# A hybrid decoder step on one core: norm inputs without a scaled copy, other orders at the seams between layers, and a routing stage whose norm, row scaling and gather are cut differently

## What is computed

```python
def rmsnorm(x, g):
    xf = x.astype(F32)
    y = xf * lax.rsqrt(jnp.mean(xf * xf, axis=-1, keepdims=True) + EPS) * g.astype(F32)
    return y.astype(x.dtype)

def short_conv_mix(xn, buf, w_in, conv_w, w_out):
    b, c, h = jnp.split(xn @ w_in, 3, axis=-1)
    u = c * h
    ...
    return (b * y) @ w_out, u_ext[:, -(CONV_W - 1):]

def swiglu(x, w1, w3, w2):
    return (jax.nn.silu(x @ w1) * (x @ w3)) @ w2

def moe_swiglu(x, router, w1, w3, w2):
    logits = (xt @ router).astype(F32)
    top_v, top_i = lax.top_k(logits, TOP_K)
    gates = jax.nn.softmax(top_v, axis=-1)
    ...
    for e in range(N_EXPERTS):
        out = out + combine[:, e:e + 1] * swiglu(xt, w1[e], w3[e], w2[e]).astype(F32)
```

## Time and profile before

| what | value |
|---|---|
| median of 3 runs | 1589.92 us (1587.15 to 1593.22) |
| the profiled execution's own time | 1587.53 us |
| its span | 1585.8 us |
| PE busy (matmul) | 1499.7 us, 95% |
| DVE busy | 1239.5 us, 78% |
| ACT busy | 954.3 us, 60% |
| POOL busy | 66.5 us, 4% |
| HBM | 305 GB/s over the span |

### The profile page before, as it was taken

The page is one execution under the profiler, slowest core; times in us unless marked ns, Lnnn a source line. Parts: engine busy times, 40 slices in busy tenths (PEclk is TensorE's granted clock), DMA queues, the critical chain, the costliest instruction groups (busy, mean ns, idle before and its releaser), DMA issues.

```text
span 1585.8 us, 23285 instructions
## 1 busy us (share of the span) xinstructions
PE 1499.7 (95%) x8758; PEld 1307.8 (82%) x8759; DVE 1239.5 (78%) x886; ACT 954.3 (60%) x671; POOL 66.5 (4%) x61
## 2 busy tenths in 40 slices
PE   6998699999989979999999999999999999999992
PEld 5987689999979978888888888888888888888881
DVE  5898665655657759888888888888888888888883
ACT  4644244334334347777777777777777777777761
POOL 1033400000000011000000000000000000000001
PEclk9999899999989989999999999999999999999997
DMA  7645377888726539999999999999999999999962
GB/s 269 194 154 163 124 280 268 297 312 312 248 102 200 167 99 400 395 393 374 377 380 370 377 379 370 377 384 360 389 375 362 383 382 357 385 381 362 380 240 96
DMA packets 212938, 484.49 MB, mean 306 GB/s; under 512 B 8810, under 2 KB 26314, under 8 KB 209820
## 3 DMA queue, kind: packets, MB, share of 16 engines
q1 hardware_dynamic: 209080, 473.67, 82.4%
q10 hardware_dynamic: 2532, 5.84, 1.0%
q0 software_dynamic: 1280, 4.33, 0.7%
HBM read 446.45 MB, written 37.40 MB: 305 GB/s over the span
## 4 chain that ended last, share of the span: by engine, by line
PE 82%; DVE 4%; issue 1%; ACT 1%; DMA 1%; POOL 0%; POOLq 0%; ACTq 0%; DVEq 0%
PE Q L2166 20%; PE Q L2122 13%; PE Q L2120 13%; PE Q L2121 13%; PE Q L1737 7%; PE Q L1738 7%; PE Q L1739 7%; PE Q L2151 2%; DVE wlo L1020 1%; DVE sr L1054 0%; PE Q L2101 0%; DMA back<-y_rows,idx 0%; PE Q L2130 0%; DVE xl L1046 0%; DVE xn L1041 0%
## 5 line engine op out<-in xcount | busy, mean ns | idle before, releaser
L1020 DVE TENSOR_TENSOR wlo<-raw,whi 128x2048 fp32r<-128x2048 f32 x414 | 940.3, 2289 | 207.0 <-ACT whi L887 121.1
L887 ACT ACTIVATE whi<-raw 128x2048 fp32r<-128x2048 f32 x336 | 643.1, 1921 | 185.0 <-PE Q L2122 85.4
L2120 PE MATMUL Q<-whi,xgh 128*128 128x512 f32 x896 | 357.5, 399 | 2.4 <-issue 2.4
L2122 PE MATMUL Q<-whi,xgl 128*128 128x512 f32 x896 | 353.8, 395 | 0.0
L2121 PE MATMUL Q<-wlo,xgh 128*128 128x512 f32 x896 | 352.8, 394 | 0.0
L1737 PE MATMUL Q<-xh,whi 128*128 128x264 f32 x1024 | 298.3, 291 | 14.7 <-DVE xl L1046 6.3
L1738 PE MATMUL Q<-xl,whi 128*128 128x264 f32 x1024 | 295.5, 289 | 0.0
L1739 PE MATMUL Q<-xh,wlo 128*128 128x264 f32 x1024 | 294.1, 287 | 0.0
L1737 PEld LDWEIGHTS Q<-xh,whi 128*128 128x128 f32 x1024 | 197.4, 193 | 17.4 <-issue 15.6
L2120 PEld LDWEIGHTS Q<-whi,xgh 128*128 128x128 f32 x896 | 169.3, 189 | 38.1 <-issue 2.6
L2122 PEld LDWEIGHTS Q<-whi,xgl 128*128 128x128 f32 x896 | 169.2, 189 | 37.6
(11 more groups left out here) (231 smaller groups left out, 1099.1 us busy)
## 6 DMA issues: line engine op xcount, KB each, us to landing
raw<-in_moe_w SPq DMA_DIRECT2D x336, 1024.0 KB, 7.6
raw<-in_ffn_w SPq DMA_DIRECT2D x42, 1024.0 KB, 6.9
raw<-in_hgrn_w_in SPq DMA_DIRECT2D x16, 1024.0 KB, 6.4
xg_rows<-zeros SPq DMA_DIRECT2D x6, 2048.0 KB, 10.8
y_rows<-zeros SPq DMA_DIRECT2D x6, 2048.0 KB, 10.8
raw<-in_conv_w_in SPq DMA_DIRECT2D x12, 1024.0 KB, 6.0
st<-in_state_hgrn SPq DMA_DIRECT2D x8, 512.0 KB, 4.4
raw<-in_hgrn_w_out SPq DMA_DIRECT2D x4, 1024.0 KB, 5.1
```

What stands on the lines that cost most here:

```text
L887: a.activation(bufs(q)[0], raw[:, n % RAW, PW * (q % 2):PW * (q % 2 + 1)], ACT.Copy).then_inc(hi_done, 1)
L1020: v.tensor_tensor(low, raw[:, slot, PW * half:PW * (half + 1)], high.bitcast(F32), ALU.subtract).then_inc(lo_done, 1)
L2120: t_.matmul(out, xgh[:, kt, :], high[:, w], start=(kt == 0), stop=False)
L2122: mm = t_.matmul(out, xgl[:, kt, :], high[:, w], start=False, stop=(kt == DT - 1))
```

## The change

1. **Norms.** `half_ready` no longer writes `xn`. `high_half` makes each tile of `xh` from xT with the norm weight as ACT's scale (4 instructions of 128 x 264 for a half instead of 1 of 128 x 1056), `low_half` makes each tile of `xl` as xT times weight minus xh (4 DVE instructions instead of 1). `add_squares` is two additions (528 and 264 wide) in place of the strided reduction. `sum_squares` moves from behind the first half of the product into its second half (before its third group; for mix0 before its first).
2. **Start.** ACT copies both halves of x and splits piece 0 between them; the router's load goes behind the first six pieces; the bounds `lbs` are worked out before the norm's root.
3. **SP.** `chunk(C_FFN, ...)` goes behind `in_state(7)`.
4. **Output projection to dense layer.** `high_out(1, 2)` and `low_out(1, 2)` go ahead of the splits; the second half of the norm goes behind the first half's and one split.
5. **Dense layer to convolution.** `last_down` runs over the two pieces outside and the two groups of outputs inside, waiting for one piece at a time; the last `ffn_add(i, 1)` goes ahead of the split; the next product's first two pieces are split ahead of the norm.
6. **cg** is turned between the halves of cin5, in Q[0].
7. **Routing.** cout1 is added to xT by tiles as its groups finish. The row norm comes from squares of xT by features (`row_squares`, `add_row_squares`) that PE sums by 6 products with ones (`sum_rows`). The lower 512 features of xs are multiplied by the weight on POOL (from xr) and by 1/rms on ACT, the upper 512 made by DVE straight from PSUM. The gather runs by halves of the features into Q[0] banks 2 and 3, and xgh, xgl are made by halves; the first piece's split goes ahead of the index arithmetic.

```diff
@@ SP
             in_state(4)
-            chunk(C_FFN, kp(ffn_w1[0])[:, :, 0:FW])
             out_state(sp, 2)
             in_state(6)
             out_state(sp, 3)
             in_state(7)
+            chunk(C_FFN, kp(ffn_w1[0])[:, :, 0:FW])
             in_state(5)
@@ ACT
-                act.wait_ge(sem("xn_" + which), 4 * j + 4)
-                a.activation(xh[:, 4 * j:4 * j + 4, :], xn[:, 4 * j:4 * j + 4, :], ACT.Copy
-                             ).then_inc(sem("xh_" + which), 1)
+                act.wait_ge(sem("x_ready_" + which), j + 1)
+                for d in range(4 * j, 4 * j + 4):
+                    n = VN[which] + d
+                    a.activation(xh[:, d, :], xT[:, d, :], ACT.Copy, scale=vecs[:, n:n + 1]
+                                 ).then_inc(sem("xh_" + which), 1)
...
+            split_to(2 * C_CIN + 1)
+            split_to(2 * C_CIN + 2)
             for j in range(2):
                 high_half("mix1", j)
+            for j in range(2):
                 squares("mix1", j)
-                split_to(2 * C_CIN + 1 + j)
+            split_to(2 * C_CIN + 3)
             root("mix1")
...
+            row_squares(0)
+            early(1)
+            row_squares(1)
             act.wait_ge(used, 2 * C_COUT + 4)
+            rows_out(0)
+            act.wait_ge(sem("squares_summed"), len(NORMS) + 1)
+            for r, ts in ((P, slice(0, BLK)), (B, slice(BLK, TT))):
+                a.activation(tk[0:r, 10, ts], quad("xt")[0:r, 3, ts], ACT.Sqrt, bias=eps[0:r, :], scale=1.0 / D
+                             ).then_inc(sem("rt_ffn1"), 1)
+            act.wait_ge(sem("rstd_ready"), 1)
+            for t in range(TT):
+                r = rows[t]
+                act.wait_ge(sem("xs_gained"), t + 1)
+                a.activation(xs[0:r, t, 0:512], xs[0:r, t, 0:512], ACT.Copy, scale=tk[0:r, 11, t:t + 1]
+                             ).then_inc(sem("xs_low"), 1)
             early(2)
@@ DVE
+            def low_half(which, j):
+
                 for d in range(4 * j, 4 * j + 4):
...
+                    v.scalar_tensor_tensor(out=xl[:, d, :], in0=xT[:, d, :], scalar=vec(which, d),
+                                           in1=xh[:, d, :].bitcast(F32), op0=ALU.mult, op1=ALU.subtract
+                                           ).then_inc(sem("xl_" + which), 1)
...
-                v.tensor_reduce(r[:, j, :], q[:, 4 * j:4 * j + 4, :].rearrange("p d t -> p t d"),
-                                AX.X, ALU.add).then_inc(sem("squares_added"), 1)
+                n = 4 * j
+                then(v.tensor_tensor(q[:, n:n + 2, :], q[:, n:n + 2, :], q[:, n + 2:n + 4, :], ALU.add))
+                v.tensor_tensor(r[:, j, :], q[:, n, :], q[:, n + 1, :], ALU.add
+                                ).then_inc(sem("squares_added"), 1)
...
+            low_out(1, 2)
             split_to(20)
-            low_out(1, 2)
             add_out(0, 1)
@@ PE
+            def last_down(base):
+
+                pe.wait_ge(sem("fl_ready"), FB)
+                for half in range(2):
+                    pe.wait_ge(lo_done, base + half + 1)
+                    for j in range(2):
+                        pe.wait_ge(sem("x_added"), 2 * FB - 1 + j)
...
             def route(j):
...
+                for d in range(4 * j, 4 * j + 4):
+                    if j == 1:
+                        pe.wait_ge(sem("x_ready_ffn1"), d - 2)
...
+                    sum_rows()
...
+            for half in range(2):
+                for t in range(TT):
+                    r = rows[t]
+                    pe.wait_ge(sem("pm_ready"), t + 1)
+                    pe.wait_ge(sem("xs_ready") if half else sem("xs_low"), t + 1)
```

More of the change, by code:

```diff
@@ L906, in _ @@
                 for t in range(TT):
-                    r = rows[t]
-                    a.activation(xs[0:r, t, 512 * j:512 * (j + 1)], row_half(t, j), ACT.Square,
-                                 accum_out=tk[0:r, 9 + j, t:t + 1]).then_inc(sem("row_squares"), 1)
-                if j == 0:
-                    early(1)
-            act.wait_ge(sem("ss_rows"), 1)
-            a.activation(tk[:, 10, :], tk[:, 9, :], ACT.Sqrt, bias=eps[:, :], scale=1.0 / D
-                         ).then_inc(sem("rt_ffn1"), 1)
@@ L1508, in _ @@
                         step(p + 2)
-                    low_half("cout", j)
-            for c in range(2):
-                if c == 0:
-                    step(2 * C_COUT)
-                    step(2 * C_COUT + 1)
+                    low_cout(j)
+            step(2 * C_COUT)
+            step(2 * C_COUT + 1)
+            then(v.tensor_tensor(xT[:, 0:4, :], xT[:, 0:4, :], quad("cout0")[:, :, 0:T], ALU.add))
+            dve.sem_inc(let_go("cout0"), 2)
+            dve.sem_inc(sem("x_ready_ffn1"), 1)
@@ L1599, in _ @@
             dve.sem_inc(sem("idx_ready"), 1)
-            then(v.tensor_copy(cnt[:, :], quad("route")[:, 0, TT * E:(TT + 1) * E]))
-            dve.sem_inc(sem("ranks_read"), 1)
-            early(1)
-            gathered(0)
+            gathered_half(1)
             early(2)
@@ L2053, in route, with sum_rows @@
+            def sum_rows():
+                pe.wait_ge(sem("squares_added"), 2 * len(NORMS) + 2)
+                for j in range(2):
+                    for t in range(TT):
+                        r = rows[t]
+                        mm = t_.matmul(quad("xt")[0:r, 3, t:t + 1], sqx[:, 4 * j, P * t:P * t + r], ones[:, 0:1],
+                                       start=(j == 0 and t == 0), stop=(j == 1), skip_group_check=True)
+                mm.then_inc(sem("squares_summed"), 1)
             def route(j):
```

303 lines of the change are left out of this document (180 added, 123 removed).

## The result

| | changed | before, same chip |
|---|---|---|
| median | 1547.86 us (1547.37 to 1551.68, 4 executions) | 1588.79 us (1587.15 to 1593.22, 4 executions) |
| profiled execution | 1547.37 us, span 1545.6 | 1587.53 us, span 1585.8 |
| PE busy | 1488.3 us, 96% | 1499.7 us, 95% |

The ratio is 0.9745, with a 95% interval of 0.9733 to 0.9756: 40.9 us faster. The forecast was 1551 us in a range of 1541 to 1565, with a chance of 0.93 for faster: right. The forecast's sum was 38.9 us; the two profiled executions differ by 40.2. Of the 3.1 us between 1551 and 1547.86, 1.2 are this sum and 1.9 the step from the profiled execution to the median, for which the forecast added 2.4 us and the changed kernel shows 0.5.

A forecast was written before the change was run, and what follows sets the result against it. PE, busy 1499.7 of 1585.8 us, was taken as the bound, with only its idle or slow time to win. Six terms summed to 38.9 us: 1548.6 from the profiled execution, 1551 us as median, range 1541 to 1565.

The forecast's parts named there:

- Start: Kernel start: ACT splits piece 0 before the norm weights arrive, first product at about 17.6 us; gain 3.3 us.
- Rival B: Norms: ACT's steps, as large as 0.6 us each, set the pace, costing 6 us in all; 1557 us, chance 0.10.
- State loads: SP's weights behind the state loads: POOL's decays start earlier, PE's 7.5 us wait for the spread goes; gain 8.8 us.
- Output projection to dense: Seam from output projection to dense layer: waits for xl and the sum of squares shrink or go; gain 9.2 us.
- Dense to convolution: Seam from dense layer to convolution: PE's waits for splits and half clock go, 1.2 us left; gain 12.1 us.
- Conv state: Conv state's transposes, between the halves of cin5, no longer wait 1.6 us for a bank; gain 1.6 us.
- Routing and entry: Routing and expert entry: PE starts expert 0 5.3 us earlier but is held at first transposes by DVE; gain 3.9 us.
- the rows' lower half passes POOL (3 x 1.0): Routing: the rows' lower half passes POOL (3 x 1.0) and ACT (3 x 0.75) before PE asks.
- Term 2: State loads, with SP's feed-forward weights moved behind them; gain 8.8 us, bounds 0 and 9.2.

The follow-up runs named there:

- experiment 9: Changed kernel with the exponential of the top two logits moved from the expert stage's entry to its end; 1552.60 us, ratio 0.9782.
- experiment 10: Changed kernel with DVE's first product of silu and gate moved ahead of two of its four splits; 1550.76 us, ratio 0.9762.
- experiment 1: Changed kernel with SP again issuing the first feed-forward weights ahead of the stores and loads of states; 1561.35 us, ratio 0.9835.
- experiment 2: Kernel before the change with only SP's state order moved (feed-forward weights behind the states); 1577.84 us, ratio 0.9933.
- experiment 7: Changed kernel with the dense layer's sum of squares again between the two halves of its first projection; 1554.38 us, ratio 0.979.
- experiment 4: Changed kernel with the scaled copy xn back in the three norms, all orders new; 1557.15 us, ratio 0.9813.
- experiment 5: Changed kernel with the strided sum of squares (tensor_reduce) in place of the two adds in the three norms; 1553.77 us, ratio 0.9786.
- experiment 3: Changed kernel with the old orders at the end of the dense layer, the norm's new instructions kept; 1562.00 us, ratio 0.9839.
- experiment 8: Changed kernel with DVE making the rows' lower half from PSUM, without POOL's multiply and ACT's scaling; 1551.79 us, ratio 0.9773.
- experiment 12: Changed kernel with PE waiting for xl by pieces, plus 40 unread products in PE's gaps ahead of the gather; 1549.09 us, ratio 0.9747.

## Why the prediction was right, step by step

**Start: right, in parts that cancel, and the equal number is luck.** The same code gave 4.5 and 4.1 in experiments 9 and 10. The first product came at 17.89, not 17.6. I had taken 0.53 us for each of ACT's four steps from the nearest row. The group measured:

```profile
L641 ACT ACTIVATE xh<-xT,vecs 128x264 fp32r<-128x264 f32 x24 | 10.4, 507 | 13.6 <-DVEq L1081 13.5
```

10.4 us for 24 is 0.43 a step, and a group of four took 1.74, not the 2.1 of my row, whose instruction has a bias beside the scale. Rival B falls with it. The Trainium skill ("VectorE: DVE Perf Modes", the section on the TRN2 errata) gave an estimated 1.6 for the four, and the trace lies near it with 1.74. Against that, x landed late in this execution: kernels with the same start had their first product as early as 17.17. No experiment takes back the start's own edits, so their share is read from positions alone.

**State loads: right.** Experiments 1 and 2 show the mechanism from both sides, and experiment 2 gives the 8.8 itself. The 1.4 by which the profile of the full change exceeds it are the half clock from 159.8 to 163.2 us of the kernel before, which this profile lacks and experiments 2, 9 and 10 have. The decays began at 145.03, not near 150, since head 5's load, the last in the queue, had landed by then, and they took 5.61 us, not the 7.65 of my row. But the gate behind them waited 2.65 us for ACT.

**Output projection to dense: right, 0.7 too small.** I left waits of 1.6 and 1.1 us; the first measured 1.3 and the second did not arise. The second half of xl was ready at 194.65 us, about when PE asked, and not at 195.5 as my 209.0 says for this trace; ACT's shorter steps are 0.4 of that, and the rest is not broken down. Experiment 7 shows what the place of the sum is worth (2.2 us), experiment 4 the norm's (2.0), experiment 5 the adds' (1.1).

**Dense to convolution: right, 0.5 too large.** The wait ahead of the convolution is 0.9 us (I said 1.2), the one ahead of the last W2 product is gone. The gain is by the orders (experiment 3).

**Conv state: right**, 2.1 for 1.6.

**Routing and entry: mechanism right, 1.2 too large.** PE starts expert 0 4.5 us earlier (I said 5.3) and is held at its first transposes, as forecast. The step that failed is "the rows' lower half passes POOL (3 x 1.0)" as if it cost nobody else: it stretches three steps of DVE by 2.5 us (experiment 8). DVE ended the row scaling at 548.4, where my 583.3, less the 37.0 won by then, says 546.3, and its first htl stands 2.1 us nearer and not 3.9. Even so POOL was no bad place for the rows: with DVE making them, experiment 8 wins at most 0.4. That DVE binds there fits experiments 9 and 10. The other edits of the routing (the norm's detour, the gather by halves) were not taken back one by one.

What the sum did not foresee is where it lost and won clock. The start had won 4.3 us by 88 us; its first products came up to full clock sooner, too, 3.8 us behind the first where the kernel before took 5.9. Behind the short waits at 120.9, 123.1 and 124.7 us the granted clock was 0.50 up to 130.9, while in the kernel before the half clock (125.7 to 132.5 us) was over when the same twelve products came: they are 0.22 us apart instead of 0.12, 1.2 us in all. So 3.3 are left in the table. Term 2 won 1.4 back, by the half clock that this profile lacks. Both are a matter of where a stretch of half clock falls, and both come out differently in experiments 9 and 10, whose code is the same there. That they nearly cancel is luck, and the sum of 38.9 against 39.7 is better than its parts.

## What to carry to other kernels

Cut waits in front of the bounding engine at the place where the last one ends, and read the clock behind them: at the end of the dense layer orders (what is split and summed ahead of what) were worth 13.9 us and the shorter norm instructions 2.8 and 0.6 on top of them, and one of the orders pays only together with the others. A step given to an idle engine is free only if it shares nothing with the engine that it relieves. Where differences of a few microseconds are asked for, compare positions of the same instruction in two traces, part by part; a total mixes them with clock falls that the edit did not make. And have a second trace of the same code before a term is read to 1 us.

## What the runs showed of the hardware

- POOL's multiply of two SBUF tiles stretched DVE's instructions with two SBUF inputs from 0.43 to 1.46, from 0.18 to 0.69 and from 0.18 to 1.16 us, each until just behind the end of the multiply that it met, and left others alone (experiment 8). The other way round, a decay of POOL that met a split on DVE took 3.94 us instead of 1.90 (experiment 1).
- The same 48 products of the gather took 6.2 us in seven kernels of the new form (with experiment 12, eight), 8.3 in one and 10.4 to 10.5 in three, at a granted clock of 0.50, even where the code ahead of them is the same (experiments 9 and 10). In experiment 9 it cannot be the edit's doing, which stands behind the gather, and it moves a total by some 4 us.
- The clock fell to 0.5 near 530 us in six of the twelve experiments with PE busy in every microsecond; it did not in the changed kernel's profile. It cost 1.6 us each time. In all six it began 2.8 to 3.5 us behind the first of the 24 records of products of 8 columns, among the 12 turns that follow them. What decides it stays open, since they stand in the runs without a fall too.
